# Clearing the experts' output rows behind the modulation's pieces, and a score wait on the emptied bank

## The reference

```
mod_l = split(silu(c) @ mod_w[i] + mod_b[i], 6)           # also mod_c from c_ctx: shifts, scales and gates
hl = rms_norm(xl, norm_mix[i]) * (1 + mod_l[1]) + mod_l[0]
# layer 0, for each of 16 heads and each latent query:
s_nb  = q @ k_window * scale + bias;  s_ctx = q @ k_context * scale
p = softmax(concat(s_nb, s_ctx));     o = p @ v
xl = xl + mod_l[2] * (o @ w_o)
...
y = zeros_like(h).at[tok].add(expert outputs * gate)
```

## Time and profile before

| | us |
|---|---|
| median of 3 runs | 4276.66 |
| lowest and highest | 4273.02 and 4281.04 |
| profiled execution, its own time | 4282.49 |
| profiled execution, span | 4280.8 |
| mean granted TensorE clock | 0.938 of full speed |

### The profile page before, as it was taken

How to read it: one execution, slowest core, us unless ns; L and a number is a source line. 1 busy time by engine, 2 the same in 40 slices (tenths; PEclk the granted TensorE clock), 3 DMA queues, 4 the chain that set the end, 5 groups by cost and what they waited for, 6 DMA issues and landing times. The chain is left out here.

```text
span 4280.8 us, 54593 instructions
## 1 busy us (share of the span) xinstructions
PE 3830.7 (89%) x22796; PEld 2936.6 (69%) x22796; DVE 1191.5 (28%) x3087; ACT 776.1 (18%) x1688; POOL 497.1 (12%) x497
## 2 busy tenths in 40 slices
PE   4799999989399999999948999999795899999994
PEld 2556667645377899998725666666543789997873
DVE  3133333322210111111164555555513101011114
ACT  1122333321000000000022333333310000000001
POOL 3100000014200000000061111011023100000003
PEclk7899999999699999999969999999996999999997
DMA  6864001111554467779541000000104555679994
GB/s 180 350 234 155 24 20 28 40 41 44 178 163 133 164 201 243 259 264 308 199 142 31 16 16 16 16 16 11 45 25 145 179 166 193 206 258 308 313 311 164
DMA packets 451177, 621.05 MB, mean 145 GB/s; under 512 B 27552, under 2 KB 346544, under 8 KB 444672
## 3 DMA queue, kind: packets, MB, share of 16 engines
q1 hardware_dynamic: 420952, 516.45, 36.7%
q0 software_dynamic: 22240, 73.58, 4.7%
q10 hardware_dynamic: 7752, 27.59, 1.7%
HBM read 550.54 MB, written 67.40 MB: 144 GB/s over the span
## 5 line engine op out<-in xcount | busy, mean ns | idle before, releaser
L1672 PE MATMUL ps<-item_xT,expert_ring 128*128 128x128 f32 (+9 forms) x8192 | 1168.8, 306 | 1.1 <-DVE item_xT L1749 1.1
L1672 PEld LDWEIGHTS ps<-item_xT,expert_ring 128*128 128x128 f32 x8192 | 1114.9, 191 | 57.2 <-issue 5.7
L1705 PE MATMUL ps<-item_aT,expert_ring 128*128 128x144 f32 (+8 forms) x2304 | 408.7, 333 | 0.0
L1756 DVE TENSOR_TENSOR item_aT<-item_silu,ps 128x128 f32<-128x128 f32 (+9 forms) x256 | 83.7, 327 | 1068.6 <-ACT item_silu L1726 1068.6
L1705 PEld LDWEIGHTS ps<-item_aT,expert_ring 128*128 128x128 f32 x2304 | 359.7, 193 | 24.9 <-issue 1.5
L1726 ACT ACTIVATE item_silu<-ps 128x128 f32<-128x128 f32 (+9 forms) x256 | 79.0, 309 | 1313.6 <-PE ps L1672 1313.6
L729 PE MATMUL ps<-hT,w_group 128*128 128x512 f32 (+1 forms) x704 | 255.9, 517 | 0.4 <-PEq L292 0.4
L374 PE MATMUL ps<-hT,oT 128*128 128x512 f32 x576 | 251.6, 597 | 1.4 <-PEq L979 0.7
L1071 PE MATMUL ps<-hT,w_group 128*128 128x512 f32 (+1 forms) x576 | 232.3, 546 | 0.4 <-PEq L292 0.4
L1622 POOL DMA_INDIRECT gathered<-h_rows,slot_idx x55 | 52.5, 954 | 1523.6 <-PE ps L1655 1513.1
L1767 DVE COPY item_y<-ps 128x512 f32<-128x512 f32 (+3 forms) x106 | 69.0, 684 | 573.5 <-PE ps L1685 396.6
(11 more groups left out here) (206 smaller groups left out, 4086.8 us busy)
## 6 DMA issues: line engine op xcount, KB each, us to landing
expert_ring<-in_expert_w_gate SPq DMA_DIRECT2D x128, 1024.0 KB, 5.3
expert_ring<-in_expert_w_up SPq DMA_DIRECT2D x128, 1024.0 KB, 8.2
expert_ring<-in_expert_w_down SPq DMA_DIRECT2D x64, 2048.0 KB, 9.6
oT<-in_mod_w SPq DMA_DIRECT2D x40, 1024.0 KB, 7.5
slot_out<-rows POOLq DMA_DIRECT2D x7, 4096.0 KB, 47.6
w_group<-in_w_qkv SPq DMA_DIRECT2D x48, 512.0 KB, 3.8
slot_out<-item_y ACTq DMA_DIRECT2D x35, 512.0 KB, 7.5
h_rows<-hr SPq DMA_DIRECT2D x18, 512.0 KB, 2.6
```

The lines of the kernel that those rows point to most:

```text
L1672: m = nc.tensor.matmul(gub(j, b, w), ring[:, b // 2, k, w * 256 + (b % 2) * P:w * 256 + (b % 2 + 1) * P], xT[:, k, 0:C], start=k == 0, sto ...
L1705: m = nc.tensor.matmul(yb(j, d), ring[:, 4 + d // 4, f, (d % 4) * P:(d % 4 + 1) * P], aT[:, f, 0:C], start=f == 0, stop=f == FB - 1)
L1756: nc.vector.tensor_tensor(aT[:, b, 0:C], sg[:, b % 2, 0:C], gub(j, b, 1), ALU.mult).then_inc(s_a, 1)
```

## The change

Two edits, both in `neighbourhood`.

1. GpSimd no longer issues the eight clearing DMAs at the stage's start. It makes the tables of groups 0, 1 and 2 (the latter two unrolled), waits until 37 of the 40 pieces of mod_w are used (2 * NPIECE - RING = 37), issues the eight DMAs, and then runs its loop over groups 3 to 7.
2. `scores(g, i)` waits on `s_pre` instead of `s_nm`, with the same count: until `biased` of the step before has read the score banks, not until `normalised` of the step before has scaled the probabilities.

```
-                    for n in range(0, rest.shape[1], 16):
-                        m = min(16, rest.shape[1] - n)
-                        pool.dma_start(rest[:, n:n + m, :], zeros.unsqueeze(1).to_broadcast([P, m, HALF])).then_inc(s_cleared, 16)
-
                     def tables(g, first):
...
                     tables(0, True)
-                    with pool.Fori(1, GROUPS) as g:
+                    for g in range(1, 3):
+                        tables(g, False)
+
+                    pool.wait_ge(s_half, 2 * NPIECE - RING)
+                    for n in range(0, rest.shape[1], 16):
+                        m = min(16, rest.shape[1] - n)
+                        pool.dma_start(rest[:, n:n + m, :], zeros.unsqueeze(1).to_broadcast([P, m, HALF])).then_inc(s_cleared, 16)
+                    with pool.Fori(3, GROUPS) as g:
                         tables(g, False)
                     pool.wait_ge(s_cleared, CLEARS * 16)
...
-                        pe.wait_ge(s_nm, g * 2 * NS + 2 * i)
+                        pe.wait_ge(s_pre, g * 2 * NS + 2 * i)
```

## The result

| | before | after |
|---|---|---|
| median of the runs, us | 4278.8 (4 runs, 4273.0 to 4281.0) | 4231.8 (4 runs, 4229.6 to 4235.0) |
| span of the profiled execution, us | 4280.8 | 4227.9 |

The ratio is 0.9893, 95% interval 0.9876 to 0.9910: 47.0 us faster by the medians, where 42.6 were forecast (4234 us, range 4222 to 4256). The forecast stood on a median of 4276.7 us from three executions; the fourth moved it to 4278.8, which is 2.1 of the 4.4 us between the two gains. In the kernel after, code lines behind the two edits are shifted by up to three: L769 is L772, L810 is L813, L870 is L873, and the clearing is L720.

A forecast was written before the change was run, and what follows sets the result against it. TensorE was taken to bound the kernel, busy 89% of the span, with piece and score waits to win. 20.8 + 1.2 - 3 + 2.9 + 10.4 + 10.3 = 42.6 us; 4276.7 - 42.6 = 4234 us, range 4222 to 4256.

The forecast's parts named there:

- The first pieces: Stage start: without the clearing, the first three mod_w pieces land before TensorE wants them; gain 20.8 us.
- the small waits: Remaining piece waits within the old clearing's flood, apart from the ends of groups 0 and 1, go; gain 1.2 us.
- Piece 39: End of group 1: the moved clearing slows the last mod_w piece to 10.7 us; loss 3 us, bounds 0 and 20.
- Rival D: The last mod_w piece starves until the clearing ends, landing about 97 us after issue; 4320 us, slower; chance 0.04.
- The start: Scores(2) run before the scaling ends, so the transposes start earlier; gain 2.9 us, bounds 1.3 and 3.6.
- Boundaries: Where groups begin: scores follow the values without idling, at the fast clock; gain 10.4 us, lower bound 5.3.
- last group: Last group's step falls from 6.26 to 5.0 us, VectorE's own loop; gain 10.3 us, bounds 7 and 11.3.
- rival A: The clock falls anyway and piece 39 is slow: gain only 31 us, 4246 us; chance 0.15.
- B: End of group 1: ScalarE's loop jump waits for instructions during the clearing, losing 14.5 us; 4248 us; chance 0.08.
- C: Stage start: first pieces are late anyway because SP's small loads stall for their own sake; 18 us, 4259 us; chance 0.05.
- no piece wait before 280 us: Sign of being right: TensorE waits for no mod_w piece before 280 us.
- The cover of the clearing: Behind the moved clearing, tables of group 3 and weight loads have time to spare, about 60 us per weight load; loss nothing.

The follow-up runs named there:

- the run of edit 1: The kernel after with the old score wait put back, so only the clearing is moved: 4257.4 us, ratio 0.9948 to before.
- the run at 34: The kernel after with the clearing issued three pieces earlier (wait for 34 in place of 37): 4244.8 us, ratio 0.9925 to before.

## Why the prediction was right

**The first pieces: 20.8 forecast, 21.1 and 21.5 measured; the small waits 1.2, measured 1.6.** Both by the comparison with the same step one group later. That this comes from the clearing and not from SP's order is shown by the run with the pieces first; that it needs edit 1 alone, by the run of edit 1 (12.8 us in the stretch). I put L185's 18 us down as the cause of the lateness; it was a sign of it. The cause was the queue's rate.

**Piece 39: loss 3 forecast, 1.5 measured by the wait, 0.2 to 2.8 by the stretch.** Its landing was 9.2 us (10.7 forecast) and the wait 4.25 in place of 2.71. The direction of the reason was right, the room to the edge was not seen: the flood needs a moment to start after GpSimd's issue (in the kernel before, issue at 120.37, 10 GB/s from 121 to 122 us, 299 from 122 to 123), and with the flood already there the same piece takes 21.6 us. By the rule of turns I had given a piece half the rate. That fits a piece by itself, whose packets are as large as the clearing's (10.0 us in the run at 34), but not the weights ahead of it. Rival D was thus nearer in mechanism than its 0.04 said, but its price is 13 us and not 89.

**The start: 2.9 forecast, 4.0 to 4.6 measured.** This term was too small, since I left the clock low. Without the 3.6 us of idle time scores(2) take 1.36 us, before 2.51, and the transposes behind them 1.12, before 1.97.

**Boundaries: 10.4 forecast, 8 to 11 measured; last group: 10.3 forecast, 11 to 13 measured.** The step became 4.91 us (5.01 forecast). Here I did count on the fast clock, and it came where the scaling had been the only wait: rival A did not. (At the end of group 3, where TensorE has "issue" time, the scores still take 2.50 us, at 548.70 in the kernel after.) The transposes took over the wait, and VectorE's loop sets the step, as said.

**Rivals B and C.** ScalarE's idle time at the jump is 10.64 us, ended by TensorE (10.60 in the earlier trace rows). Two instruction packets moved in the flood between 374 and 375 us, and no engine stood idle for them. The Trainium skill (Runtime: NRT & Kernel Launch, "Instruction fetch mechanics") says that a taken branch out of the two pages held forces a DMA for the target page. What fits it here is TensorE at the end of group 3, where its loop jumps back: 2.86 and 1.02 us of "issue" stand in the kernel after, as 2.76 and 1.36 did before, and two instruction packets move between 542 and 546 us, where the first of them stands. That these are the fetch is argued, not tested; the flood is over by then, so no run shows such a stall under load. C is out: the first pieces land by 153 us.

**The signs.** One sign of being right did not come as written: "no piece wait before 280 us". The wait for piece 19, which the sum let stand, was at 288 in the kernel before and came at 257 in the kernel after, because all ahead of it had become shorter. For the same reason the clearing was issued at 358 and not near 365.

**The cover of the clearing.** Forecast at nothing, and so measured, but for one step of the reasoning only by luck: I weighed what stands behind the clearing in GpSimd's queue by the 8.9 us of its issue. That holds for eight DMAs; for a ninth it would have been 78 us.

**Sum.** 42.6 forecast, 47.0 by the medians; by the trace the stage from the first L738 (L741) to w_o is 775.2 and 768.4 us before, 723.5 and 724.3 after, so 44 to 52 us. About half of the missing 4 us is the median that the forecast stood on; the stretches show a gain that was set too small at the start (by 1 to 2 us, the clock) and in the last group (by 1 to 3), and a loss for the last piece that was set too large (by up to 3). The term of the boundaries was 1 too small by one pair of profiles and 3 too large by the other.

## What to carry to other kernels

A bulk transfer that nobody needs yet is not free in the background: it slows every queue that shares the DMA engines, most of all loads with short rows and whatever stands behind them. Start it behind the last load that an engine waits for, and look at what stands behind it in its own issuing queue. A wait should name what the instruction really needs (the bank emptied), not the last thing that happens after it; where work fills the gap it is worth nothing, where the pipeline has no filler it is worth nearly the instruction's whole duration on each step (here 1.35 us of 6.26). Two such edits can hide each other: the gain of the score wait was 5 to 6 us larger once the clearing no longer held the DMA behind it.

## What the runs showed of the hardware

- Two busy DMA queues moved equal numbers of packets (3933 and 3889 in 44 us), at 4.0 KB against 0.49 KB each: 15.9 MB against 1.9.
- GpSimd issued eight DMAs of 4 MB (the last 1 MB) in 8.9 us, and was held 78 us at the ninth, until the eighth had landed.
- SP too is held at the issue: eight loads of 4 KB took 18.1 us to issue in the flood, 2.5 without it, and one piece of 1 MB took 11.4 us.
- In the kernel after, two weight loads issued at 400.4 and 428.3, in the flood, landed after 17.0 and 18.9 us, where the median of all such loads is 3.9.
- The granted clock is the main scatter here: the same stretch at the end of group 0 took 16.5 and 20.0 us in two executions of the kernel before (0.7 of it in the wait for the piece), and behind the idle 1.55 us of a boundary the scores ran at the lower level (2.50 us), without it at the higher (1.36). In the last group the same 1.55 us left them at the higher.
